# Sample attention of a hybrid decoder step: value products in four column groups of 32 rows and 128 columns, a PSUM bank per sample

## The reference, cut to what matters

```python
def dilated_sample(q, k_all, v_all, n_buf):          # mixer A, per pattern
    ...
    s = jnp.einsum('bthe,btjhe->bthj', q, kg, preferred_element_type=F32) * scale
    p, lse = softmax_stats(s, valid)
    o = jnp.einsum('bthj,btjhe->bthe', p, vg.astype(F32))
    ...
    return merge_by_denominator(parts)
```

## Time and profile before

| | us |
|---|---|
| three runs, median | 2371.94 (2360.09 to 2373.01) |
| the profiled execution, its own time | 2370.07 |
| the profiled execution, its span | 2368.6 |
| sample attention in it, from the first key transposes to the barrier | 262 to 638 |
| PE busy, over the whole span | 2071.5 (87%) |
| DVE, ACT busy | 564.4 (24%), 385.8 (16%) |

### The profile page before, as it was taken

One profiled execution on the slowest core, in us unless ns is written; L12 is line 12 of the kernel. 1 busy time (PEld: TensorE's weight loads), 2 busy tenths in 40 slices (PEclk: granted clock), 3 DMA queues, 4 the chain that ended last, 5 costly groups with the idle time before them and its releaser, 6 DMA issues. The chain is left out here.

```text
span 2368.6 us, 52730 instructions
## 1 busy us (share of the span) xinstructions
PE 2071.5 (87%) x22769; PEld 1391.3 (59%) x22769; DVE 564.4 (24%) x1208; ACT 385.8 (16%) x937; POOL 98.5 (4%) x185
## 2 busy tenths in 40 slices
PE   6979489788789999898797767899999999999975
PEld 4755355454367777666566755666766676665643
DVE  2023253353220000103255433211112111111103
ACT  2014233222110000102132211110111011010001
POOL 0000012112100000000000000000000000000001
PEclk9989699889899999997698668999999999999987
DMA  8339689999862241347321030968987979989794
GB/s 273 107 118 359 174 259 345 271 300 322 257 225 98 80 145 51 107 154 252 89 70 32 13 93 20 378 263 338 377 321 279 346 288 353 350 331 408 267 402 162
DMA packets 286396, 537.47 MB, mean 227 GB/s; under 512 B 31045, under 2 KB 78082, under 8 KB 286172
## 3 DMA queue, kind: packets, MB, share of 16 engines
q1 hardware_dynamic: 272198, 491.50, 59.0%
q0 software_dynamic: 12960, 41.43, 5.0%
q10 hardware_dynamic: 1014, 1.27, 0.2%
HBM read 520.70 MB, written 13.44 MB: 226 GB/s over the span
## 5 line engine op out<-in xcount | busy, mean ns | idle before, releaser
L2416 PE MATMUL PS<-moe_ring,moe_X 128*32 128x256 f32 (+1 forms) x5376 | 295.4, 368 | 22.0 <-DMA moe_ring<-in_moe_w 16.7
L2436 PE MATMUL PS<-moe_ring,moe_HT 128*32 128x256 f32 x4224 | 264.0, 382 | 4.0 <-issue 2.7
L2416 PEld LDWEIGHTS PS<-moe_ring,moe_X 128*32 128x32 f32 x5376 | 181.1, 112 | 122.0 <-issue 19.2
L415 PE MATMUL PS<-H,w_ring 128*128 128x320 f32 x768 | 215.6, 443 | 17.1 <-DMA w_ring<-in_w_out_even 6.7
L2416 PE MATMUL PS<-moe_ring,H 128*32 128x256 f32 (+1 forms) x3840 | 206.0, 363 | 6.6 <-issue 4.2
L415 PEld LDWEIGHTS PS<-H,w_ring 128*128 128x128 f32 x768 | 149.2, 195 | 80.5 <-DMA w_ring<-in_w_out_even 6.8
L1137 PE MATMUL PS<-H,ffn_ring 128*128 128x320 f32 x704 | 191.6, 435 | 3.5 <-ACT H L240 3.5
L833 PE MATMUL PS<-ident,KV 128*128 128x128 f32 x832 | 123.3, 312 | 72.8 <-DMA KV<-in_cache_win_kv 24.9
L2436 PEld LDWEIGHTS PS<-moe_ring,moe_HT 128*32 128x32 f32 x4224 | 143.6, 111 | 69.7 <-issue 8.2
L2416 PEld LDWEIGHTS PS<-moe_ring,H 128*32 128x32 f32 x3840 | 126.1, 110 | 75.8 <-issue 7.1
L1137 PEld LDWEIGHTS PS<-H,ffn_ring 128*128 128x128 f32 x704 | 134.8, 192 | 60.1 <-issue 4.7
(11 more groups left out here) (470 smaller groups left out, 1935.8 us busy)
## 6 DMA issues: line engine op xcount, KB each, us to landing
moe_ring<-in_moe_w SPq DMA_DIRECT2D x168, 1024.0 KB, 10.4
moe_ring<-in_moe_w SPq DMA_DIRECT2D x40, 2048.0 KB, 15.6
ada_ring<-in_ada_w SPq DMA_DIRECT2D x24, 2048.0 KB, 15.3
KV<-in_cache_win_kv SPq DMA_DIRECT2D x128, 256.0 KB, 8.5
KV<-in_cache_moba_kv POOLq DMA_DIRECT2D x128, 256.0 KB, 6.4
KV<-in_cache_moba_kv SPq DMA_DIRECT2D x128, 256.0 KB, 8.3
ffn_ring<-in_ffn_w SPq DMA_DIRECT2D x14, 2048.0 KB, 12.8
moe_ring<-in_moe_w SPq DMA_DIRECT2D x32, 512.0 KB, 7.5
```

The source lines that it names most:

```text
L415: last = pe.matmul(PS[0:width, banks[g % B], 0:TOK], RING[:, n % R, k, m:m + width], rhs[:, k, :], start=(k == 0), stop=(k == KT - 1))
L2416: mm = pe.matmul(PS[32 * j:32 * j + 32, i % 2, 0:2 * w].rearrange("p (a n) -> p a n", a=2), X[:, k, UNIT * u:UNIT * (u + 1)], RING[:, slot ...
L2436: mm = pe.matmul(PS[32 * g:32 * g + 32, 3, 0:256], HT[:, i % 2, 32 * j:32 * j + 32], rows[:, 256 * g:256 * (g + 1)], start=(j == 0), stop= ...
```

## The change

Value products are formed in four column groups. For each tile, sample s and group i (two heads) there is one product: stationary the 32 columns of group i (two heads of both samples), moving the 128 value columns of these two heads. The sums of sample 0 go to bank 6, those of sample 1 to bank 7, 128 columns each. In each bank half of a group's rows are of the other sample; the mask drops them along with the other head of the two. A tile and sample thus have four products of 128 columns in place of one of 512.

What follows from it: `PT` keeps the transposes' own layout, so ACT copies a bank at once. `OD` and the mask have 256 columns instead of 512, `own_head` reads both banks, `outputs` has two products instead of four, and `TSEL` has 32 columns instead of 16. Bank 7 is also one of the two banks of the probabilities; so PE, ahead of each group of probabilities for bank 7, waits until `own_head` has read the sums that stood there.

```diff
-        PT = [sb("PTA", [P, NT[0], 2, 64]), sb("PTB", [P, NT[1], 2, 64])]
+        PT = [sb("PTA", [P, NT[0], 4, 32]), sb("PTB", [P, NT[1], 4, 32])]
...
-        OD = [sb("ODA", [P, 512]), sb("ODB", [P, 512])]
+        OD = [sb("ODA", [P, 256]), sb("ODB", [P, 256])]
...
-        HM = sb("HM", [P, 512])
-        TSEL = sb("TSEL", [P, 2 * DT])
+        HM = sb("HM", [P, 256])
+        TSEL = sb("TSEL", [P, 4 * DT])
...
                         ge(pe, p_out, NPT, b, P0[m] + max(j - 1, 0))
+                        if PBANK[j % 2] == OBANK + 1:
+                            ge(pe, od_done, 2, b, m)
                         apart(pe)
...
                     def product(rows, t, s, v, start, stop):
-                        return pe.matmul(PS[64 * s:64 * s + 64, OBANK, :], PT[m][0:rows, t, s, :], v, start=start, stop=stop)
+                        for i in range(4):
+                            mm = pe.matmul(PS[32 * i:32 * i + 32, OBANK + s, 0:P], PT[m][0:rows, t, i, :], v[:, P * i:P * i + P], start=start, stop=stop)
+                        return mm
...
-                    for i in range(4):
-                        mm = pe.matmul(PS[:, OBANK, i * 2 * DT:(i + 1) * 2 * DT], OD[m][:, i * P:(i + 1) * P], TSEL[:], start=True, stop=True)
+                    for s in range(2):
+                        mm = pe.matmul(PS[:, OBANK, s * 4 * DT:(s + 1) * 4 * DT], OD[m][:, s * P:(s + 1) * P], TSEL[:], start=True, stop=True)
...
-                        bank = PS[:, PBANK[j % 2], :].rearrange("k (t i s x) -> k t s i x", t=4, i=4, s=2)
-                        for s in range(2):
-                            if t1 > t0:
-                                last = copy(PT[m][:, t0:t1, s, :].rearrange("k t (i x) -> k t i x", i=4), bank[:, 0:t1 - t0, s])
-                            if j == -(-NT[m] // 4) - 1:
-                                last = copy(PT[m][0:64, NT[m] - 1, s, :].rearrange("k (i x) -> k i x", i=4), bank[0:64, (NT[m] - 1) % 4, s])
+                        bank = PS[:, PBANK[j % 2], :].rearrange("k (t i x) -> k t i x", t=4, i=4)
+                        if t1 > t0:
+                            last = copy(PT[m][:, t0:t1], bank[:, 0:t1 - t0])
+                        if j == -(-NT[m] // 4) - 1:
+                            last = copy(PT[m][0:64, NT[m] - 1], bank[0:64, (NT[m] - 1) % 4])
...
-                    dve.tensor_tensor(OD[m][:], PS[:, OBANK, :], HM[:], ALU.mult).then_inc(od_done, 1)
+                    dve.tensor_tensor(OD[m][:].rearrange("p (s n) -> p s n", s=2), PS[:, OBANK:OBANK + 2, 0:P], HM[:].rearrange("p (s n) -> p s n", s=2), ALU.mult).then_inc(od_done, 1)
...
-    t["head_mask"] = (np.arange(512)[None, :] // HD == row % 64 // DT).astype(f)
-    t["token_select"] = (np.arange(2 * DT)[None, :] == DT * (row // 64) + row % DT).astype(f)
+    t["head_mask"] = (np.arange(2 * P)[None, :] // HD == row % 32 // DT).astype(f)
+    t["token_select"] = (np.arange(4 * DT)[None, :] == DT * (row // 32) + row % DT).astype(f)
```

More of the change, by code:

```diff
@@ L947, in outputs @@
                     where = bass.ds(b * n + (SEQ - n * back), n)
-                    copy(H[:, 4 * m:4 * m + 4, where], PS[:, OBANK, 0:4 * n].rearrange("p (i t) -> p i t", t=n)).then_inc(o_out, 1)
+                    copy(H[:, 4 * m:4 * m + 4, where].rearrange("p i (s t) -> p s i t", s=2), PS[:, OBANK, 0:4 * n].rearrange("p (s i t) -> p s i t", s=2, i=4)).then_inc(o_out, 1)
                 def body(b, last):
```

## The result

The changed kernel takes 2351.93 us, the median of seven runs (2349.91 to 2359.82), beside 2371.94 for seven of the kernel before: a ratio of 0.9941, interval 0.9914 to 0.9968, some 14 us less (8 to 20). The ratios leave out runs that fell into a slower state, here one of 4110.54 us among the seven before, while the medians count every run. The forecast was 2361.6, 10.3 us less than before; the measured median lies 0.9 us inside the lower end of its range. The profiled execution took 2357.34, its span 2355.8.

A forecast was written before the change was run, and what follows sets the result against it. The sample attention was taken as one stream of loads that PE interrupts three times, plus a tail. 0.4 + 2.2 + 2.65 + 2.65 + 0.5 + 2.4 - 0.5 = 10.3 us less gave 2361.6; range 2351 to 2370.

The forecast's parts named there:

- (4) of the costs: PE, idle longer before keys, may restart at the lower clock: 0 to 2 us, taken as 0.
- The slower rival: Value products: if column groups don't stream side by side, a record costs 110 ns, the whole 2418 us; chance 0.04.
- the conversion of dips into time: Sample attention: earlier slot releases counted as time won, 2.2, 2.65, 2.65 and 0.5 us.
- dips: Sample attention at 336 to 346, 462 to 478, 554 to 568 us: DMA at 0.73, 0.59, 0.69 while PE multiplies values.
- dip 2: Sample attention, 462 to 478 us: DMA share 0.59, costing 6.9 us, of which 2.65 counted as won.
- The term of 0.5 us: PE's longer program: instruction packets could go from 13 to 19, costing 0.5 us of the load stream.
- The loop's turn: SP's back edge, iteration 1 to 2, in the sample attention: reason for not counting the rest of dip 2.
- SP's gap: In dip 2 SP issues two loads from 465.35 us on and its next only at 474.82.
- all dips close: Sample attention: SP reaches its back edge early, the stream never starves; 18.6 us less in sum, 2353; chance 0.15.
- All later stages the same length: Expected sign: the sample attention ends some 10 us earlier, and the stages behind it keep their length.
- the rival of PE's program: Rival from the experiments: the length or place of PE's program shortens stages behind the sample attention; no chance given.

The follow-up runs named there:

- thin loads: Either kernel, ended after the sample attention, each ring load cut to 128 of its 512 columns: 616.88 us for the kernel before, 594.58 for the changed.
- the split kernel: The kernel before with each value product split into four of 128 columns, same stationary operand: 2380.2 us, ratio 1.0040.
- the unrolled kernel: The changed kernel with SP's and POOL's loads of pairs 1 and 2 written out instead of a loop: 2354.87 us, ratio 0.9940.
- the repeat: The changed kernel run once more without an edit: 2356.16 us, ratio 0.9939 to the kernel before.
- the ended one: The changed kernel ended after the sample attention, all later stages left out: 635.62 us, ratio 0.2671 to the whole kernel before.
- the kernel before (repeat): The kernel before run once more without an edit: 2372.51 us.
- the one with two queues: The changed kernel with mixer A's loads shared by SP and POOL: 2363.83 us, ratio 0.9983 to the kernel before.

## Why the prediction was near, and where it failed

**PE's side was nearly right.** At the full granted clock a tile takes 16 x 30.6 = 0.49 us (0.44 forecast, 0.86 before), and with thin loads PE saves 47.5 us (48 forecast). own_head, the new tokens' products and ACT's copies measured near what was worked out. With full loads PE saves some 40 us, and the term that missed is the lower clock, (4) of the costs, put at 0. It was feared ahead of keys, but the values lose most by it: behind the stop at 345.62 the granted clock was 0.53 and a record took 55 ns (5.13/93). A's values take 27.6 us in the changed kernel and 19.8 with thin loads, where the kernel before has 39.0 and 35.2. The slower rival (groups that take turns) is refuted by 30.6 ns a record. The Trainium skill (TensorE: Matmul & The Clock Gate, section "Wait — 56ns, not 53.3ns?") speaks of some 62 ns a matmul without hardware decode. The records of the change don't show it, at 30.6 ns. The 66 ns of the split kernel lie near it; why its records cost 66 is open (PE's weight loads fill 5.79 of the 6.00 us from 339 to 345 there, and their part was not tested).

**The step that failed is the conversion of dips into time.** The prediction took a share of 1.04 as full speed, and each released microsecond of a dip as one off the end. The dips were filled by even more than it said: 10 x 0.33 + 16 x 0.25 + 14 x 0.28 = 11.2 us of the engines' time, beside 7.5. The stage then needed nearly as long as before, because the same bytes kept the engines busy longer. The queues from 255 to 637 us (packets, MB, share of 16 engines), before and after:

```profile
q1 hardware_dynamic: 42704, 76.74, 69.2%
q0 software_dynamic: 10240, 33.56, 25.2%
```

```profile
q1 hardware_dynamic: 42706, 76.62, 70.9%
q0 software_dynamic: 10240, 33.56, 25.6%
```

From 94.4 to 96.5% of 382 us is 8 us more of packets, for 0.1 MB less. Over the three profiles of each kernel the mean rises from 94.9 to 97.1%, and the highest, 97.9, belongs to the unrolled kernel whose dip 2 is filled best. A share of 1.04 to 1.06 stands beside 252 GB/s in one stretch of the table after and 330 in another: it says that packets are under way, not that they move at a fixed rate. What made the packets longer is not shown. So the 10.3 us put into the stage came out as 4 to 6 in the kernels that end there, and as 1.6 between the profiles.

**Code fetch was mis-sized.** The term of 0.5 us looked only at the stream. Instruction packets did go from 13 to 20, as said (though its base of some 370 products a pair has no row: the stage's 2032 records are 254 a pair). But PE itself stood still for 7.7 us (5.6 in the repeat), in pair 0 and the loop's first pass. That this is the fetching of code is argued, not shown. For it: the changed kernel, its repeat, the unrolled and the ended one all stop behind the same 67th record of A's values of pair 0, for 3.2 to 4.6 us. With thin loads the stop is gone, so the full stream of loads is part of its cause. The Trainium skill (Runtime: NRT & Kernel Launch, section "Instruction fetch mechanics") holds that fetch is hidden, since instructions are issued more slowly than blocks arrive. If the stops are fetches, the rows at 345.62 and 382.06 disagree with it under full loads, and the row at 337.92 agrees under thin ones. The longest stop, 4.34 us, lies under A's values, where DVE's queries come late anyway (PE waits another 1.60 us for them behind it), so little of it is lost.

**The loop's turn was a doubtful reason for a right restraint.** The prediction left 4.2 us of dip 2 out because of SP's gap. The gap was there, and unrolled it is gone and the time unchanged. The rival "all dips close" thus has its condition nearly met in that kernel, and not its price; but PE stood 10 us more there without a visible reason, so why the price failed is open.

**"All later stages the same length" was wrong for the profiles compared.** Most of their 13 us lies behind the stage. Retention alone gives 3.9 in the mean, and it has two lengths, 93.5 and 98 to 100. The timeline of the kernel before (repeat), then of the changed one, around the point where they part:

```profile
1100.42 1.92 PE L148 MATMUL PS<-ada_ring,CT 128*32 128x512 f32 x16 [0.89 <-DMA ada_ring<-in_ada_w]
...
1107.66 2.05 PE L1293 MATMUL PS<-d_VN,d_KN 128*128 128x128 f32 x16
...
1112.84 9.28 PE L1302 MATMUL PS<-d_VN,d_KM 64*128 64x128 f32 x48 [1.14 <-DVE RS_new L1385]
```

```profile
1093.23 1.92 PE L148 MATMUL PS<-ada_ring,CT 128*32 128x512 f32 x16
...
1102.34 3.18 PE L1296 MATMUL PS<-d_VN,d_KN 128*128 128x128 f32 x16
...
1108.06 5.92 PE L1305 MATMUL PS<-d_VN,d_KM 64*128 64x128 f32 x48 [0.56 <-DVE RS_new L1388]
```

The table by stretches around it, again the repeat of before and then the changed kernel (granted clock, DMA share and GB/s stand last):

```profile
1096.00:1106.00 10.00, 8.49 (x69) 5.23 (x70) 1.61 (x2) 4.66 (x9) 0.00 (x0) 1.00 1.04 383
...
1116.00:1126.00 10.00, 10.00 (x46) 9.43 (x45) 2.77 (x5) 0.00 (x0) 0.00 (x0) 0.50 0.22 61
```

```profile
1100.00:1110.00 10.00, 9.44 (x60) 8.37 (x58) 5.24 (x10) 4.86 (x6) 0.00 (x0) 0.76 0.33 115
1110.00:1120.00 10.00, 10.00 (x75) 9.43 (x74) 3.44 (x5) 0.00 (x0) 0.00 (x0) 0.92 0.43 124
```

The work is the same. In the kernel before PE had waited 0.89 us for a load; the clock stays at its upper level, 2.4 GHz, over the short products (2.05) and is granted at 0.50 of it, 1.2 GHz, from the 48 long ones on (9.28 us). In the changed kernel it falls over the short ones (3.18) and is back for the long ones (5.92). Of eight profiles of whole kernels three show the short form: the changed kernel, its repeat, and the split kernel, which is slower than either. In these the products against ada_ring at the head of the rows start 33.4 us behind the stage's barrier; in the five long forms, the unrolled changed kernel and the one with two queues among them, 34.0 to 34.9. So the form goes neither with PE's program nor with the speed of the sample attention; 0.6 us ahead of this point goes with 5 behind it. That delay isn't always a load: in the unrolled changed kernel all of it was there before the first of these products. Whether the change shifts these moments for good, or the profiles fell so, is open. The 4.4 us of the experts are not explained either; there the stalls without visible cause and the waits for weights vary by as much from one profile to the next. All eight profiles together keep the rival of PE's program alive: what lies behind the stage took 1726.6 to 1730.3 us in the three with PE's shorter program, and 1714.5 to 1723.2 in the five with a longer one (the split kernel 1717.8, the two-queue kernel some 1721). One profile for each kernel does not show it either.

What is settled: the whole gains 14 us (interval 8 to 20), the sample attention by itself some 4 to 6 (0 to 11), and a stage freed of most of its loads gives 22. What is open: how much of the difference between 14 and 4 to 6 is more than the spread of two measurements whose intervals overlap. The total came out within 10 us of the forecast and inside its range, but that is partly luck: the stage gave less than the sum had for it, and the rest came from stages where the sum had nothing. The changed kernel remains the fastest version run, level with its unrolled form.

## What to carry to other kernels

Where an engine and a stream of loads are near balance, sum the engine's saving against its new waits (here 40 saved, against 36 in loads and 8 in stops). An idle share of the DMA engines isn't time to be won unless the GB/s of the busy stretches are one rate: look at both columns. To learn what a saving would give without the loads, cut columns, not partitions, and look at the DMA share of the cut kernel before using it.

## What was not expected of the hardware

- Loads that fill half of the partitions kept the DMA share at 0.80 to 0.88 for 174 to 183 GB/s in two stretches; loads of a quarter of the columns brought it to 0.34 at 94.
- A stretch at a DMA share of 1.05 moved 245 GB/s where two queues carried much of A's cache, one at 1.06 moved 252 with one queue; another at 1.04 moved 330.
- PE stood still for up to 4.34 us, for no reason that the profile shows, in straight-line code of 128-column records at 30.6 ns each, for 0.5 at most with records of 66 ns, and not at that place with records of 28.6 ns under thin loads.
- A 128-column record took 30.6 ns among four column groups of 32 columns, and 66 ns with 64 stationary columns, both at the full granted clock; behind a stop, at 0.53 of it, 55 ns in the column groups.
- The same work of a stage took 93.5 us or 98 to 100, as the granted clock fell to 1.2 GHz over short products or over long ones; a start 0.6 us later went with the long form in all eight profiles.
